# Expert weights of a two-layer mixture of experts: slot 1's first loads behind the first gather, its loads in a round one by one

## The chip, the cores and the metric

The kernel runs on one core of a Trainium2 chip. The time is that of the whole program on the device, in microseconds (us). A core has TensorE (PE, matrix products), VectorE (DVE), ScalarE (ACT), GpSimd (POOL) and SyncE (SP), each with its own instruction stream; SP, ACT and POOL also issue DMAs, and all DMAs of the core run on the same 16 DMA engines. Everything here is float32.

## The reference, cut to what matters

The program is two transformer-like blocks over 1024 tokens of width 1024. The change touches only the mixture of experts, which runs twice (`l` = 0 and 1, in the second block):

```python
def moe_ffn(h, w_rg, b_rg, w_re, b_re, w_gate, w_up, w_down):
    # routing: one of 4 groups, the 2 best of its 8 experts, a gate weight for each
    ...
    order = jnp.argsort(flat_e)              # 2048 (token, expert) pairs sorted by expert
    ...
    xb = h[row_tok].reshape(n_blocks, MOE_BLOCK, d)
    def expert_block(args):
        xblk, e = args
        hid = jax.nn.silu(xblk @ w_gate[e]) * (xblk @ w_up[e])
        return hid @ w_down[e]
    yb = lax.map(expert_block, (xb, block_e)).reshape(n_rows, d)
    return jnp.zeros_like(h).at[row_tok].add(yb * row_w[:, None])
```

There are 32 experts; each has 1024 x 512 gate and up matrices and a 512 x 1024 down matrix, together 6.3 MB.

## The kernel before

**Blocks and rounds.** The 2048 pairs are cut into blocks of 64 rows of one expert each. A *round* computes two blocks, one in *slot 0* and one in *slot 1*. The blocks are ordered so that slot 0 keeps its expert over several rounds (on average two), while slot 1's expert is loaded anew in every round. Layer 0 has 25 rounds and layer 1 has 24. A slot holds one expert as three parts of 2 MB each: half *a* and half *b* of the gate and up weights (each covers half of the contraction) and the *down* part. In the whole run ACT issues 98 half loads and 49 down loads for slot 1, SP 42 and 21 for slot 0.

**A round on PE** (`blocks_pe`): for slot 0, then slot 1: 16 matmuls on half a, 16 on half b (line 2314); then two transposes of slot 0's hidden rows (2321), eight transposes that turn the next round's gathered tokens (2298, `turn_x`), two transposes for slot 1, and 16 down matmuls for each slot (2331). PE waits for each half by itself (`self.wa`, `self.wb`) and for each down part (`self.wd`). When its last matmul on a part is done it raises `free_a`, `free_b` or `free_d`; each counts slot 0 and slot 1 in turn, from 2, so that `free_b >= 2*j+3` means that slot 0's half b is done in round `j`, and `2*j+4` slot 1's.

**Who loads what.** SP runs `blocks_sp` and reloads slot 0 as its parts come free. ACT has the loads of slot 1 in its own stream, in program order with its other work (`round_act`): Silu for slot 0, Silu for slot 1, a copy of half of the turned tokens (`copy_x`), the two half loads for the next round, the copy of slot 0's result, the two stores of it to `y_tok`, the two stores of slot 1's result (which DVE copies, `ye[1]`), the down load. POOL gathers the next round's 128 token rows from `h_tok` in DRAM (0.5 MB) once PE has turned the current ones (`blocks_pool`).

**Start of a layer.** Stages are closed by all four compute engines (`close`): the next stage begins on an engine when every engine has closed the last. In stage `m0_route` (`m1_route`), ACT ends `route_act` with slot 1's first three loads, each half held until slot 0's same half has landed (`landed[0], 32`), and closes the stage behind them. POOL's first gather is the first thing of the next stage, `m0_blocks`. SP does not take part in the closing; it issues slot 0's first loads as soon as the table of blocks is there (`m_tg`).

## Time and profile before

| | us |
|---|---|
| median of 3 runs | 4514.99 (4512.74 to 4518.06) |
| the profiled execution | 4513.96 |
| its span | 4512.1 |
| round stages, first to last expert matmul of slots and down, layer 0 | 2594.2 to 3236.3 |
| the same, layer 1 | 3829.3 to 4435.9 |

The page of the profile gives PE 88% of the span, DVE 32%, ACT 20%, POOL 3%. In its table of 40 slices, the two stages of experts (slices 23 to 29 and 34 to 40) are where the DMA engines are busiest, at 8 or 9 tenths in most slices. In the rows below, a line number such as L2314 is a line of the kernel before; L2267 issues a half load, L2272 a down load, L2348 a store, L2284 the gather. "Idle before" in brackets is the time the engine sat idle before the instruction, and who ended it.

### The profile page before, as it was taken

Reading aid. Unit: us, or ns where it says so; the run is one execution under the profiler, and the core shown is the slowest. Engines: PE = TensorE matmul, PEld = TensorE weight load, DVE = VectorE, ACT = ScalarE, POOL = GpSimd, SP = SyncE. Lnnn points to the kernel's source line nnn. Section 1 sums busy time; section 2 is a strip of 40 time slices with the busy share of each in tenths; the row PEclk is TensorE's granted clock in tenths of the full one; section 3 lists DMA queues with packets and bytes.
Section 4 is the critical chain, followed back from the end, with each engine's and each line's share of the span. In section 5 each row is a group of like instructions: output and inputs, shape, how many; then the busy total and the mean of one; then the engine's idle time right before and its main releaser. Section 6 shows DMA issues by size and latency. Waiting matters only on the chain. (4 is left out here: it accounts for less than half of the span.)

```text
span 4512.1 us, 48953 instructions
## 1 busy us (share of the span) xinstructions
PE 3960.7 (88%) x19350; PEld 1982.4 (44%) x19351; DVE 1440.6 (32%) x2699; ACT 898.9 (20%) x1891; POOL 122.8 (3%) x199
## 2 busy tenths in 40 slices
PE   4997888899998889999778599889799995999895
PEld 2564665454444554453554333333344443333333
DVE  2486666213204661431553311111231123111114
ACT  3003445102002331300451211111120012111111
POOL 0000000000000000000000000000100000000001
PEclk8998999999999999999999799999899997999997
DMA  6311223001100000110320389999811003899995
GB/s 248 121 38 38 95 101 125 28 22 38 55 37 19 1 1 28 47 47 37 133 102 2 153 322 375 404 401 406 316 36 38 37 20 158 322 395 379 408 404 208
DMA packets 81279, 693.44 MB, mean 154 GB/s; under 512 B 9696, under 2 KB 11560, under 8 KB 45408
## 3 DMA queue, kind: packets, MB, share of 16 engines
q10 hardware_dynamic: 39824, 342.78, 18.8%
q1 hardware_dynamic: 23168, 280.66, 15.5%
q0 software_dynamic: 18128, 67.77, 4.2%
q8 instruction: 114, 1.87, 0.2%
q14 instruction: 45, 0.37, 0.0%
HBM read 636.11 MB, written 55.05 MB: 153 GB/s over the span
## 5 line engine op out<-in xcount | busy, mean ns | idle before, releaser
L258 PE MATMUL banks<-arena 128*128 128x512 f32 (+2 forms) x4544 | 1750.1, 548 | 57.5 <-ACTq L137 30.4
L258 PEld LDWEIGHTS banks<-arena 128*128 128x128 f32 x4544 | 842.6, 191 | 959.0 <-issue 889.0
L2314 PE MATMUL banks<-arena 128*64 128x512 f32 x3136 | 708.0, 607 | 52.0 <-DMA arena<-in_w_gu 50.0
L2314 PEld LDWEIGHTS banks<-arena 128*64 128x64 f32 x3136 | 235.6, 140 | 515.3 <-issue 440.9
L2331 PE MATMUL banks<-arena 128*64 128x512 f32 x1568 | 371.2, 624 | 50.3 <-issue 50.3
L2331 PEld LDWEIGHTS banks<-arena 128*64 128x64 f32 x1568 | 115.4, 143 | 270.6 <-issue 270.6
L1511 PE MATMUL banks<-arena 128*64 128x128 f32 x1952 | 158.3, 285 | 83.8 <-DVE arena L1524 44.2
L937 DVE SCALAR_TENSOR_TENSOR arena<-arena 128x1024 f32<-128x1024 f32 x240 | 195.9, 877 | 0.2 <-DVEq L137 0.2
L1511 PEld LDWEIGHTS banks<-arena 128*64 128x64 f32 x1952 | 102.2, 136 | 136.6 <-ACT arena L1524 71.7
L299 DVE SCALAR_TENSOR_TENSOR arena<-banks,arena 128x512 f32<-128x512 f32 (+1 forms) x72 | 51.9, 721 | 337.4 <-PE banks L258 337.4
L2399 DVE COPY arena<-banks 128x512 f32<-128x512 f32 x49 | 33.9, 691 | 393.0 <-PE banks L2331 393.0
L2395 DVE COPY arena<-banks 128x256 f32<-128x256 f32 x98 | 41.1, 419 | 366.4 <-PE banks L2321 366.4
L1442 PE MATMUL banks<-arena 64*128 64x256 f32 (+2 forms) x768 | 131.4, 473 | 25.2 <-ACT arena L1613 15.6
L1491 PE MATMUL banks<-arena 128*128 128x128 f32 x976 | 150.1, 285 | 0.6 <-ACT arena L1613 0.6
L2391 DVE TENSOR_TENSOR arena<-arena,banks 128x256 f32<-128x256 f32 x98 | 40.7, 415 | 343.9 <-ACT arena L2355 343.9
L1239 PE MATMUL banks<-arena 128*128 128x128 f32 x800 | 109.4, 285 | 34.4 <-DVE arena L1330 34.4
L1557 DVE TENSOR_REDUCE arena<-banks 128x1 f32<-128x1024 f32 (+3 forms) x144 | 135.4, 940 | 13.0 <-PE banks L1442 9.3
L270 ACT ACTIVATE arena<-banks 128x512 f32<-128x512 f32 (+1 forms) x43 | 24.1, 559 | 577.5 <-PE banks L258 577.5
L1613 ACT ACTIVATE arena<-banks,arena 128x1024 f32<-128x1024 f32 (+3 forms) x144 | 135.3, 939 | 10.4 <-DVE arena L1559 9.4
L2355 ACT ACTIVATE arena<-banks 128x256 f32<-128x256 f32 x98 | 37.5, 383 | 495.2 <-PE banks L2314 495.2
L2355 ACT ACT_TABLE_LOAD x47 | 60.3, 1283 | 379.8 <-issue 379.8
L1491 PEld LDWEIGHTS banks<-arena 128*128 128x128 f32 x976 | 104.5, 141 | 54.1 <-issue 50.5
(341 smaller groups left out, 3105.8 us busy)
## 6 DMA issues: line engine op xcount, KB each, us to landing
arena<-in_w_gu ACTq DMA_DIRECT2D x98, 2048.0 KB, 13.9
arena<-in_w_dn ACTq DMA_DIRECT2D x49, 2048.0 KB, 17.2
arena<-in_w_gu SPq DMA_DIRECT2D x42, 2048.0 KB, 14.7
arena<-in_w_ada SPq DMA_DIRECT2D x24, 2048.0 KB, 7.3
arena<-in_w_dn SPq DMA_DIRECT2D x21, 2048.0 KB, 19.1
y_tok<-arena ACTq DMA_DIRECT2D x196, 128.0 KB, 9.9
y_tok<-arena POOLq DMA_DIRECT2D x1, 16384.0 KB, 45.2
arena<-in_ab_w_ada SPq DMA_DIRECT2D x6, 2048.0 KB, 10.4
```

The costliest lines, as they stand in the source:

```text
L258: last = pe.matmul(self.bank_of(g, n), lhsT, rhs, start=k == 0, stop=k == KT - 1)
L299: d.scalar_tensor_tensor(out=grp.dst, in0=src, scalar=grp.more["gate"], in1=grp.dst, op0=ALU.mult, op1=ALU.add).then_inc(proj_ev["D"], 1)
L937: d.scalar_tensor_tensor(out=out, in0=src, scalar=wt, in1=out, op0=ALU.mult, op1=ALU.add).then_inc(conv_n, 1)
L1239: last = pe.matmul(bank(7)[:, 0:V.shape[1]], self.PT[0:K, g % self.n_pt, 128 * j:128 * j + 128], V, start=g == mine[0] and j == 0, stop=g ...
L1442: ins = pe.matmul(banks[:, c0:c0 + k.shape[1]], q, k, start=True, stop=True)
L1491: ins = pe.transpose(self.tbank(g)[:, 128 * j:128 * j + 128], self.P[u % 2][s_][:, c0:c0 + P], ident)
L1511: ins = pe.matmul(bank(7)[64 * s_:64 * s_ + 64, 0:128], V, self.PT[g % len(self.PT)][:, 128 * j:128 * j + 128], start=g == mine[0] and j < ...
L1557: link(d.tensor_reduce(st[:, s_:s_ + 1], sc[:, 0:un["n"]], X_AXIS, ALU.max))
L1613: a.activation(self.P[i % 2][s_][:, 0:un["n"]], self.scores(s_)[:, 0:un["n"]], ACT.Exp, bias=st[:, 2 + s_:3 + s_], scale=un["scale"][s_][0 ...
L2314: last = pe.matmul(bank(2 + s_)[64 * h:64 * h + 64, :], xbT[:, k, 64 * s_:64 * s_ + 64], w_gu[s_][:, k, h], start=k == 0, stop=k == KT - 1 ...
L2331: last = pe.matmul(bank(6 + s_)[64 * h:64 * h + 64, :], hidT[:, s_, ch % 2, 64 * (ch // 2):64 * (ch // 2) + 64], w_dn[s_][:, ch, 512 * h:5 ...
L2355: a.activation(sg[:, s_], bank(2 + s_)[:, 0:256], ACT.Silu).then_inc(self.sg, 1)
```

## The change

In `route_act` the loads of slot 1 are taken out. They come at the head of the next stage, in `blocks_act`, once the first gather has landed (`xg >= 16`), without waits on slot 0's halves. In `round_act` half a is loaded when PE has freed it, between the two Silus; half b behind the second Silu; the down part between slot 0's stores and slot 1's, when PE has freed it (`free_d >= 2*j+4`).

```diff
@@ route_act
-                a.wait_ge(m_tg, l + 1)
-                e = self.expert(a, 0)
-                for part, landed in ((0, self.wa), (1, self.wb)):
-                    a.wait_ge(landed[0], 32)
-                    self.load_gu(a, 1, e, part)
-                self.load_dn(a, 1, e)
                 for tw in m_tw:
@@ round_act
-                for s_ in range(2):
-                    a.wait_ge(self.free_b, 2 * j + s_ + 3)
-                    a.activation(sg[:, s_], bank(2 + s_)[:, 0:256], ACT.Silu).then_inc(self.sg, 1)
+                a.wait_ge(self.free_b, 2 * j + 3)
+                a.activation(sg[:, 0], bank(2)[:, 0:256], ACT.Silu).then_inc(self.sg, 1)
+                if not last:
+                    a.wait_ge(self.free_a, 2 * j + 4)
+                    self.load_gu(a, 1, e, 0)
+                a.wait_ge(self.free_b, 2 * j + 4)
+                a.activation(sg[:, 1], bank(3)[:, 0:256], ACT.Silu).then_inc(self.sg, 1)
+                if not last:
+                    self.load_gu(a, 1, e, 1)
                 self.copy_x(a, "A", j + 1)
-                if not last:
-                    for part in range(2):
-                        self.load_gu(a, 1, e, part)
...
                 self.store_y(a, 0, j)
+                if not last:
+                    a.wait_ge(self.free_d, 2 * j + 4)
+                    self.load_dn(a, 1, e)
                 a.wait_ge(self.ye[1], j + 2)
                 self.store_y(a, 1, j + n)
-                if not last:
-                    self.load_dn(a, 1, e)
@@ blocks_act
+                e = self.expert(a, 0)
+                a.wait_ge(self.xg, 16)
+                for part in range(2):
+                    self.load_gu(a, 1, e, part)
+                self.load_dn(a, 1, e)
                 self.copy_x(a, "A", 0)
```

On ACT at the start of layer 0's expert stage, before: `moe0_w_half_a_slot0` counts slot 0's half a landed, `moe0_xt` the tokens turned, `stage_end` the closed stage.

```order
L2277 TENSOR_LOAD arena [waits moe_tg]
L2277 ISA x2
L2267 ISA [waits moe0_w_half_a_slot0]
L2267 DMA arena<-in_w_gu 128x4096
L2267 ISA [waits moe0_w_half_b_slot0]
L2267 DMA arena<-in_w_gu 128x4096
L2272 ISA
L2272 DMA arena<-in_w_dn 128x4096
L2244 TENSOR_LOAD arena [waits moe_tw1,moe_tw0,stage_end]
```

The same place now; the changed file's lines are numbered a little lower (2261 for 2267, 2266 for 2272).

```order
L2238 TENSOR_LOAD arena [waits moe_tw1,moe_tw0,stage_end]
L2238 ISA x2
L2373 TENSOR_LOAD arena
L2373 ISA x2
L2271 TENSOR_LOAD arena
L2271 ISA x2
L2261 ISA [waits moe0_xg]
L2261 DMA arena<-in_w_gu 128x4096
L2261 ISA
L2261 DMA arena<-in_w_gu 128x4096
L2266 ISA
L2266 DMA arena<-in_w_dn 128x4096
```

The three loads have moved from ahead of the stage's end to behind it, and from slot 0's halves to the gather as what releases them.

On ACT in the loop of rounds, before, from the first Silu to the down load:

```order
L2355 ACTIVATE arena<-banks 128x256 [waits moe0_free_b]
L2354 REGISTER_ALU
L2355 ACTIVATE arena<-banks 128x256 [waits moe0_free_b]
L2339 REGISTER_ALU
L2342 ACTIVATE arena<-banks 128x512 [waits moe0_xt]
L2267 ISA
L2267 DMA arena<-in_w_gu 128x4096
...
L2348 ISA [waits moe0_ye_dve]
L2348 DMA y_tok<-arena 64x512
L2348 ISA
L2348 DMA y_tok<-arena 64x512
L2272 ISA
L2272 DMA arena<-in_w_dn 128x4096
```

The same stretch now:

```order
L2348 ACTIVATE arena<-banks 128x256 [waits moe0_free_b]
L2350 REGISTER_ALU
L2261 ISA [waits moe0_free_a]
L2261 DMA arena<-in_w_gu 128x4096
L2353 ACTIVATE arena<-banks 128x256 [waits moe0_free_b]
L2261 ISA
L2261 DMA arena<-in_w_gu 128x4096
...
L2266 ISA [waits moe0_free_d]
L2266 DMA arena<-in_w_dn 128x4096
L2342 ISA [waits moe0_ye_dve]
L2342 DMA y_tok<-arena 64x512
```

Half a has moved ahead of the second Silu, half b ahead of the token copy, the down load ahead of slot 1's two stores. No other engine's instructions have moved.

## Rows read from the trace of the kernel before

**Rows 1.** The page: the span.

```profile
span 4512.1 us, 48953 instructions
```

**Rows 2.** Waits: engine and line, waited for; us in total, times, longest.

```profile
PE banks L2331 <- issue: 50.3, 17, 4.8
PE banks L2314 <- DMA arena<-in_w_gu: 50.0, 23, 4.8
```

**Rows 3.** Windows; columns: PE, PEld, DVE, ACT, POOL busy, PEclk, DMA share, GB/s.

```profile
2644.99:3158.76 513.77, 466.14 (x2162) 167.79 (x2160) 57.71 (x120) 64.86 (x100) 23.02 (x40) 0.97 0.97 396
3880.34:4365.88 485.54, 447.12 (x2054) 161.18 (x2052) 54.81 (x114) 61.62 (x95) 21.84 (x38) 0.96 0.96 391
3880.34:3955.86 75.52, 71.03 (x326) 24.86 (x324) 8.65 (x18) 9.73 (x15) 3.45 (x6) 0.95 0.92 374
4209.55:4261.20 51.65, 46.90 (x218) 17.43 (x216) 5.77 (x12) 6.49 (x10) 2.30 (x4) 0.97 0.99 407
3158.76:3236.50 77.74, 67.58 (x308) 25.39 (x304) 8.05 (x18) 8.45 (x14) 2.31 (x4) 0.96 0.89 372
4365.88:4436.70 70.82, 65.62 (x308) 22.99 (x304) 8.66 (x18) 8.45 (x14) 2.30 (x4) 0.98 0.86 347
2618.74:2641.14 22.40, 22.40 (x111) 8.08 (x109) 2.88 (x6) 3.24 (x5) 1.15 (x2) 1.00 0.83 327
```

**Rows 4.** Short windows of layer 1, same columns.

```profile
3867.00:3871.00 4.00, 4.00 (x26) 1.96 (x24) 1.77 (x4) 0.98 (x2) 0.81 (x2) 1.00 0.28 61
3942.00:3947.00 5.00, 5.00 (x30) 2.33 (x28) 1.77 (x4) 0.98 (x2) 1.15 (x2) 1.00 0.32 85
3906.00:3908.00 2.00, 2.00 (x8) 0.60 (x6) 0.00 (x0) 0.00 (x0) 0.00 (x0) 0.50 1.07 451
```

**Rows 5.** Timeline, start of layer 0's experts: start, us, engine, line, operation.

```profile
2562.62 0.19 DVE L2240 CAST arena<-banks 128x33 int32<-128x33 f32 x1 [1.71 <-PE banks L2054]
2562.68 1.03 SPq L2267 DMA_DIRECT2D arena<-in_w_gu  x2
2570.09 6.46 ACTq L2267 DMA_DIRECT2D arena<-in_w_gu  x2
2576.72 0.34 ACTq L2272 DMA_DIRECT2D arena<-in_w_dn  x1
2578.36 1.05 POOL L2284 DMA_INDIRECT arena<-h_tok,arena  x1 [0.87 <-POOL arena L2281]
2591.28 1.97 PE L2298 MATMUL banks<-arena 128*128 128x128 f32 x8 [28.77 <-DMA arena<-h_tok,arena]
2594.23 16.00 PE L2314 MATMUL banks<-arena 128*64 128x512 f32 x64 [0.98 <-DVE arena L2342]
```

**Rows 6.** Timeline, the same start in layer 1.

```profile
3798.48 0.19 DVE L2240 CAST arena<-banks 128x33 int32<-128x33 f32 x1 [1.71 <-PE banks L2054]
3829.31 16.27 PE L2314 MATMUL banks<-arena 128*64 128x512 f32 x64 [0.98 <-DVE arena L2342]
```

**Rows 7.** DMA issues from 3923 to 3924 us: KB each, median us to landing.

```profile
arena<-h_tok,arena POOLq DMA_INDIRECT x1, 12.2
```

**Rows 8.** The chain in order of time, one round of layer 1: start, us.

```profile
3876.66 13.73 PE banks L2314 x64
```

**Rows 9.** Timeline of the same round and the next one's stalls.

```profile
3890.44 0.38 ACT L2355 ACTIVATE arena<-banks 128x256 f32<-128x256 f32 x1 [6.48 <-PE banks L2314]
3891.82 0.86 ACTq L2267 DMA_DIRECT2D arena<-in_w_gu  x2
3898.89 3.60 PE L2314 MATMUL banks<-arena 128*64 128x512 f32 x16
3901.38 0.46 ACTq L2272 DMA_DIRECT2D arena<-in_w_dn  x1
3905.04 8.78 PE L2314 MATMUL banks<-arena 128*64 128x512 f32 x32 [2.55 <-DMA arena<-in_w_gu]
3915.76 5.35 PE L2314 MATMUL banks<-arena 128*64 128x512 f32 x16 [1.95 <-DMA arena<-in_w_gu]
```

## The prediction

> **What bounds the kernel now.** I read the page first, for the span [rows 1] and for the busiest engine, PE. The list of waits says where PE stands idle in the expert stages: PE waited 50.0 us in 23 places for halves of gate and up weights, and 50.3 us in 17 places in front of the down matmuls, where the profile names only "issue" [rows 2]; those stand in the middle of the 32 down matmuls, between slot 0's and slot 1's, so they are waits for slot 1's down part. The windows tell which resource is short. A round without a stall takes 22.40 us, with PE at 100% and DMA at 0.83 [rows 3]. From the first reload of slot 0 to the last, in both layers, the DMA engines are busy 0.97 and 0.96 of the time [rows 3]. So there are two kinds of time to win, and the reader should keep them apart: the start of each layer, where PE sits and nothing is short but order, and the steady part, where DMA is nearly full and only its idle 3 or 4% can be won.
>
> In the steady part SP reloads slot 0 every second or every third round (12 and 5 intervals). A two-round interval takes 51.65 us with DMA at 0.99 and 407 GB/s; a three-round one 75.52 us with DMA at 0.92 [rows 3]. PE would need 2 x 22.40 = 44.8 and 3 x 22.40 = 67.2 us. The idle DMA time of a three-round interval stands where slot 1 waits to be asked for: 3867 to 3871 us at a share of 0.28 and 3942 to 3947 at 0.32, so 2.9 and 3.4 us idle [rows 4]. Both end when the half loads behind the token copy start to move data. In the heavy round that follows, PE then waits 2.55 and 1.95 us, and each time runs its next matmuls at half the granted clock (0.50, the 1.2 GHz level) for a while: 16 matmuls take 5.35 us [rows 4, 9], where a quarter of 13.73 us is 3.43 [rows 8].
>
> **The start of a layer.** Before, ACT's first half load waits until slot 0's half a has landed (2570.09), its second until half b has, and the down load is issued at 2576.72. Only then does the stage close, and the gather goes out at 2578.36, 1.30 us after ACT's last issue ended (2577.06). It lands 12.9 us later, at 2591.28, behind the loads, and the first expert matmul comes 2.95 us after that, at 2594.23 [rows 5]. Now the last to close is DVE, whose last instruction ends at 2562.81. The same 1.30 us puts the gather at 2564.1. It now competes with slot 0's three loads alone. The nearest row is the gather in a light round, which had ACT's queue beside it and took 12.2 us [rows 7]; I take that, with 12.9 as the other end. So the gather lands at 2576.3, and the first expert matmul stands at 2579.3: 14.9 us earlier. Layer 1: DVE ends at 3798.67, so 3798.67 + 1.30 + 12.2 + 2.95 = 3815.1 against 3829.31, 14.2 us [rows 6]. Together 29.1 us, or 27.7 with 12.9.
>
> The cover that goes is that of slot 1's own loads: they start at about 2577, not at 2570. A load is 2.10 MB, which at 407 / 0.99 = 411 GB/s [rows 3] is 5.1 us. Slot 1's half b is the fifth load of the stage; with data moving from about 2564.7 (I allow 2 us behind SP's issue; no row here shows it), 5 x 5.1 + 1.3 for the gather ends at 2591.5. PE asks for it at 2579.3, plus slot 0's two halves (half of 13.73 plus the 16.27 - 13.73 of a slow start [rows 6, 8], 9.4 us), plus 3.43: 2592.1. That is just in time; I charge 0 to 3 us a layer and take 0.5. The down part would be there at 2596.6 and is asked for some 9 us after that half b. ACT issues three loads (about 0.5 us each) between the gather and its first token copy; PE's turning takes 1.97 us [rows 5], so they hide behind it; without that cover they would cost 1.5 us once a layer. **Start: -28 us** (-21 to -29).
>
> **In a round.** In the round of rows 8, slot 1's half a is free after three quarters of the 64 matmuls, at 3886.96. Its load was issued at 3891.82 and will be issued some 4.8 us earlier. Half b went 0.5 us behind it, at 3892.3; now it follows the second Silu (3890.44) by the 0.15 us that separated copy and load before: 1.7 us earlier. The down part was issued at 3901.38, behind two stores and DVE's copy; the last down matmul ends at about 3899.0 [rows 9], so 2.3 us earlier. A round's first load takes about 5 us of DMA, and it moves ahead by 4.8: what it does is fill the gap, and the whole train behind it comes that much sooner. In a round with stalls the gap closes altogether, since half a is asked for before PE waits for half b.
>
> What can that be worth? The idle DMA time between the first and the last reload is 0.03 x 513.77 + 0.04 x 485.54 = 34.8 us [rows 3]; more cannot be won there, since the bytes are the same. A three-round interval holds 0.08 x 75.52 = 6.0 us of it and a two-round one only 0.01 x 51.65 = 0.5. I count 80%, -28 us: in the light rounds of a three-round interval PE still needs its 22.40 us and DMA, with 0.83 of that to do, will idle a little. Of the stalls of 8.3 us in that interval (75.52 - 67.2), I expect 4 to 5 to stay, at slot 1's half b. Behind the last reload of a layer the stretches of 77.74 and 70.82 us [rows 3] stand about 13.5 and 6.5 us over what PE needs; the first has two other weight loads of the next stage on SP's queue. I count 2 and 3 us there. **Steady part: -33 us** (-15 to -48).
>
> **What is added or passed.** The wait on free_a on ACT has the second Silu behind it, which cannot start before slot 1's half b is done anyway, 3.43 us later: nothing. The wait on free_d has slot 1's stores behind it; DVE's copy that they need, which starts on the same signal, ends later still: nothing. Slot 1's stores now stand behind 2 MB on ACT's queue, so they land about 5 us later. DVE waits for them before its next copy of slot 1's result, and that copy follows 16 down matmuls (3.5 us) that themselves waited for this same down load; the stores, 0.26 MB behind it, take 0.6 us. Nothing, but with a margin of only about 3 us in a round that stalls there; beyond it each microsecond would reach ACT's next store and Silu, which has about 7 us of slack in turn. SP and POOL issue the same things; no queue is passed on them.
>
> **Sum.** 4513.96 for the profiled execution (span 4512.1 [rows 1], 1.9 us around it), minus 28, minus 33, is 4453; by rounding in the shares I say 4454. The median of the runs is 1.0 us above the profiled one, which is nothing here: a measurement of this kernel tells about 0.2%, 9 us, from no change.
>
> **Rivals.** *Only the start.* DMA is the bound and the idle slivers only move, for instance because the reordered loads arrive sooner than PE uses them and the wait passes to slot 0's parts. For it: the two-round intervals at 0.99. Against: the gaps of rows 4, which end with an issue that now comes 4.8 us sooner. Time 4513.96 - 28 = 4486. *Everything.* All 34.8 us of idle time go, the ends of both layers give 8 more and slot 1's half b is in time at the start (29): 4442, and down to 4434 if stalls that vanish take their slow matmuls with them beyond what the shares show. *Slower: half a steals from slot 0.* Where SP's and ACT's queues both hold loads they share the engines. In a heavy round ACT's half a now joins while SP's half b, which PE needs first, is still under way, for 4.8 us longer. At half the rate that puts SP's half b back by 2.4 us, and it was already 2.55 late at 3905.04 [rows 9]; with 1.9 us of slow matmuls that is 4.3 us in each of 19 heavy rounds, +82, less 28: 4568. It decides from 1.5 us lost in each heavy round on. Against it: before the heavy round the train has been moved ahead by those same 4.8 us, so ACT's queue is emptier when SP joins, and later parts gain what this one loses. *It doesn't do it.* If the gather, without the waits that staggered the loads, lands as late as before and ACT issues no sooner, because its stream is held elsewhere: about 4512.
>
> On that third case the Trainium skill has a rule, in "DMA: Bandwidth & Descriptors", section "Queues, rings and completion order": each DMA engine goes round-robin over the queues that hold work for it. By that rule the theft is real while both queues are full; whether it costs time is decided by the backlog, as above, and the profile of the change will show it. The same page's "Specifications" give about 358 GB/s as the HBM limit of a core; the two-round interval of rows 3 ran at 407, so the trace does not agree and the sum keeps to the trace. By that limit the interval's 21.0 MB would take 58.7 us, more than it did.
>
> **Chances.** Forecast (both parts, 4439 to 4472) 0.61; only the start 0.20; everything 0.12; theft 0.04; nothing 0.03. Faster by over 0.2% holds the first three, 0.93; within 0.2% 0.03; slower 0.04. The range reaches from "everything" to "only the start", 4434 to 4488.
>
> **What would show it.** Right: the first expert matmul of the stages within 17 us of SP's first load, where it was 31.6; the gather issued about 1.5 us behind SP's first issue; half a issued 0.1 us after three quarters of a round's 64 matmuls; three-round intervals of 70 to 72 us with DMA at 0.96 or more, two-round intervals of 51 us at 0.99; the waits before the down matmuls down from 50 us to under 20. Wrong: a first gather that takes over 15 us; a new wait of several microseconds in round 0 in front of slot 1's half b; waits of DVE for the stores of slot 1; two-round intervals of over 52 us with PE's longest waits in front of slot 0's half b.

## The result

| | us | |
|---|---|---|
| before, median of 4 runs | 4513.86 | 4510.16 to 4518.06 |
| after, median of 4 runs | 4441.66 | 4438.27 to 4446.76 |
| ratio | 0.9836 | 0.9824 to 0.9848 (95%) |
| forecast | 4454 | range 4434 to 4488 |

The change makes the kernel 1.6% faster: 72 us, where 60 were forecast. The spans of the two profiled executions differ by the same 72.0 us. Lines have moved in the kernel after: the gate and up matmuls stand at L2308 (before L2314), the down matmuls at L2325 (L2331), half loads at L2261, down loads at L2266, stores at L2342, the gather at L2278.

The page of the kernel after, span and costliest groups (answers to [rows 1]; columns: busy us, mean ns | idle before and what ended most of it):

```profile
span 4440.1 us, 48953 instructions
...
L2308 PE MATMUL banks<-arena 128*64 128x512 f32 x3136 | 719.6, 616 | 70.0 <-DMA arena<-in_w_gu 68.0
...
L2325 PE MATMUL banks<-arena 128*64 128x512 f32 x1568 | 349.2, 598 | 3.2 <-issue 3.2
```

Against [rows 2], the 50.3 us in front of the down matmuls have gone to 3.2 in one place. The waits for halves have grown from 50.0 to 68.0. So there are 29 us less waiting in all: nearly all of the waits for the down part have gone, and the halves take 18 us of them over.

The waits are not the whole gain in the rounds. From the first to the last expert matmul the two layers take 39 us less (1248.6 to 1209.4). Some 10 us of that are matmuls that run faster: the down matmuls are busy for 349.2 us instead of 371.2, those on the halves for 719.6 instead of 708.0. PE runs the matmuls behind a long wait at a granted clock of 0.50 for a while ([rows 4], 3906 to 3908 us), so a wait that goes takes its slow matmuls with it. The first expert matmuls of the two layers, 31 us earlier behind SP's first load, are most of the rest of the 72.

The windows of the kernel after, same columns as [rows 3]: first to last reload of slot 0 in each layer, a three-round interval, two two-round intervals, and the stretches behind the last reload:

```profile
2631.43:3124.46 493.03, 463.14 (x2162) 163.71 (x2160) 57.71 (x120) 64.44 (x101) 23.02 (x40) 0.97 0.99 413
3830.40:4298.83 468.43, 441.13 (x2054) 155.82 (x2052) 54.84 (x114) 61.64 (x96) 21.83 (x38) 0.97 0.98 406
3830.40:3904.15 73.75, 70.27 (x326) 24.79 (x324) 8.66 (x18) 9.75 (x16) 3.44 (x6) 0.95 0.94 385
4151.68:4198.85 47.17, 45.02 (x218) 16.09 (x216) 5.77 (x12) 6.44 (x11) 2.30 (x4) 1.00 1.01 424
2875.76:2926.54 50.78, 46.95 (x218) 16.41 (x216) 5.77 (x12) 6.50 (x11) 2.31 (x4) 0.97 1.01 426
3124.46:3199.77 75.31, 67.36 (x308) 24.67 (x304) 7.96 (x17) 8.33 (x14) 2.31 (x4) 0.95 0.86 360
4298.83:4365.09 66.26, 63.74 (x308) 22.69 (x304) 7.97 (x17) 8.01 (x14) 2.30 (x4) 1.00 0.83 347
```

The steady stretches fell from 513.77 and 485.54 us to 493.03 and 468.43, that is 37.8 us. The two-round interval fell too, to 47.17 us in the fourth row, though the prediction held it full at 51.65 and 0.99. Its row now says 1.01 and 424 GB/s where it said 0.99 and 407. That is 2% more share and 4% more bytes a second.

The timeline of the start of layer 0's experts, then of layer 1's (answers to [rows 5, 6]):

```profile
2562.86 0.20 DVE L2234 CAST arena<-banks 128x33 int32<-128x33 f32 x1 [1.71 <-PE banks L2054]
2562.91 1.04 SPq L2261 DMA_DIRECT2D arena<-in_w_gu  x2
...
2564.19 1.05 POOL L2278 DMA_INDIRECT arena<-h_tok,arena  x1 [0.87 <-POOL arena L2275]
...
2575.35 1.16 ACTq L2261 DMA_DIRECT2D arena<-in_w_gu  x2
...
2578.17 8.89 PE L2308 MATMUL banks<-arena 128*64 128x512 f32 x32 [0.98 <-DVE arena L2336]
...
2587.82 3.65 PE L2308 MATMUL banks<-arena 128*64 128x512 f32 x16 [0.75 <-DMA arena<-in_w_gu]
...
2593.03 3.65 PE L2308 MATMUL banks<-arena 128*64 128x512 f32 x16 [1.56 <-DMA arena<-in_w_gu]
```

```profile
3760.99 1.02 SPq L2261 DMA_DIRECT2D arena<-in_w_gu  x2
...
3777.26 13.52 PE L2308 MATMUL banks<-arena 128*64 128x512 f32 x48 [0.98 <-DVE arena L2336]
...
3792.00 3.65 PE L2308 MATMUL banks<-arena 128*64 128x512 f32 x16 [1.22 <-DMA arena<-in_w_gu]
```

The first expert matmul comes 2578.17 - 2562.91 = 15.3 us behind SP's first load in layer 0, where it was 31.6, and 3777.26 - 3760.99 = 16.3 us in layer 1, where it was 31.3. The DMA issue at 2564.19 in the timeline is the gather; its own row, against [rows 7]:

```profile
arena<-h_tok,arena POOLq DMA_INDIRECT x1, 11.0
```

Then a round without a stall, and a heavy one (answers to [rows 8, 9]):

```profile
2605.18 13.90 PE L2308 MATMUL banks<-arena 128*64 128x512 f32 x64
2605.53 0.34 ACTq L2266 DMA_DIRECT2D arena<-in_w_dn  x1
...
2615.83 0.35 ACTq L2261 DMA_DIRECT2D arena<-in_w_gu  x1
...
2619.13 0.38 ACT L2353 ACTIVATE arena<-banks 128x256 f32<-128x256 f32 x1 [6.48 <-PE banks L2308]
2619.28 0.34 ACTq L2261 DMA_DIRECT2D arena<-in_w_gu  x1
```

```profile
3848.95 10.47 PE L2308 MATMUL banks<-arena 128*64 128x512 f32 x48
...
3862.89 6.50 PE L2308 MATMUL banks<-arena 128*64 128x512 f32 x16 [3.48 <-DMA arena<-in_w_gu]
```

Half a is issued 10.65 us after the first matmul of the round. The start of the same kind of round before is read from the same view here, the timeline, which puts it 0.17 us ahead of the chain of [rows 8]:

```profile
3876.49 13.90 PE L2314 MATMUL banks<-arena 128*64 128x512 f32 x64
```

There half a was issued 3891.82 - 3876.49 = 15.33 us into the round, so it is now asked for 4.7 us sooner. Half b goes out at 14.10 us, and the down part 0.35 us into the next round. The heavy round has one wait, at its last 16 matmuls, which are slot 1's half b.

The windows of a light round of layer 1 in which a gap is left (answers to [rows 4]); the gap now ends with half a's load, issued 10.65 us into the round:

```profile
3886.00:3888.00 2.00, 2.00 (x12) 0.71 (x10) 0.00 (x0) 0.00 (x0) 0.00 (x0) 1.00 0.13 48
3888.00:3890.00 2.00, 2.00 (x12) 0.65 (x10) 0.00 (x0) 0.00 (x0) 0.00 (x0) 1.00 0.53 106
```

Cut into slots of 2 us, the steady stretches (first to last reload of slot 0) show how much each kernel left unused. I take a slot that moves under 200 GB/s as one in which the queues ran dry; between 200 and 380 I expect slots with the small stores or with a short gap. "Lost" is the time that the missing bytes would take at 430 GB/s, the rate of a full slot (the median of the slots above 380 is 432 before and 426 after). The waits of PE, by the quarter of the 64 gate and up matmuls or the half of the down matmuls that they precede, are summed from the timeline.

| | slots under 200 (lost us) | 200 to 380 (lost us) | waits at slot 0's half b | slot 1's halves | slot 0's down | slot 1's down | waits in all |
|---|---|---|---|---|---|---|---|
| before | 28 (43.8) | 85 (43.3) | 13.5 | 36.6 | 0 | 50.3 | 100.4 |
| after | 10 (15.9) | 47 (21.0) | 0 | 68.0 | 0 | 3.2 | 71.2 |

### The profile page after: what moved, and what is told of

The parts are those of the page before. It is cut to its first block and busy times, and to the rows that moved or that the text cites. A ratio compares the mean times of both kernels' runs of the same rounds, so it can differ in the third digit from the quotient of the medians.

```text
span 4440.1 us, 48953 instructions
## 1 busy us (share of the span) xinstructions
PE 3953.8 (89%) x19350; PEld 1975.0 (44%) x19351; DVE 1441.2 (32%) x2699; ACT 898.7 (20%) x1891; POOL 121.7 (3%) x199
## 5 line engine op out<-in xcount | busy, mean ns | idle before, releaser
L2308 PE MATMUL banks<-arena 128*64 128x512 f32 x3136 | 719.6, 616 | 70.0 <-DMA arena<-in_w_gu 68.0
L2308 PEld LDWEIGHTS banks<-arena 128*64 128x64 f32 x3136 | 231.5, 142 | 548.2 <-issue 455.8
L2325 PE MATMUL banks<-arena 128*64 128x512 f32 x1568 | 349.2, 598 | 3.2 <-issue 3.2
L2325 PEld LDWEIGHTS banks<-arena 128*64 128x64 f32 x1568 | 108.9, 137 | 208.5 <-issue 208.5
L1511 PEld LDWEIGHTS banks<-arena 128*64 128x64 f32 x1952 | 101.9, 136 | 137.3 <-ACT arena L1524 71.7
L270 ACT ACTIVATE arena<-banks 128x512 f32<-128x512 f32 (+1 forms) x43 | 24.1, 559 | 580.3 <-PE banks L258 580.3
L1524 ACT ACTIVATE arena<-banks 128x512 f32<-128x512 f32 (+1 forms) x160 | 90.6, 566 | 168.5 <-PE banks L1491 167.1
L278 ACT ACTIVATE arena<-banks 128x512 f32<-128x512 f32 (+1 forms) x68 | 38.0, 559 | 424.1 <-PE banks L258 424.1
## 6 DMA issues: line engine op xcount, KB each, us to landing
y_tok<-arena ACTq DMA_DIRECT2D x196, 128.0 KB, 13.9
```

Source lines behind the costliest of these rows:

```text
L1511: ins = pe.matmul(bank(7)[64 * s_:64 * s_ + 64, 0:128], V, self.PT[g % len(self.PT)][:, 128 * j:128 * j + 128], start=g == mine[0] and j < ...
L1524: last = eng.tensor_copy(o, s_) if which == "D" else eng.activation(o, s_, ACT.Copy)
L2308: last = pe.matmul(bank(2 + s_)[64 * h:64 * h + 64, :], xbT[:, k, 64 * s_:64 * s_ + 64], w_gu[s_][:, k, h], start=k == 0, stop=k == KT - 1 ...
L2325: last = pe.matmul(bank(6 + s_)[64 * h:64 * h + 64, :], hidT[:, s_, ch % 2, 64 * (ch // 2):64 * (ch // 2) + 64], w_dn[s_][:, ch, 512 * h:5 ...
```

## The experiments

The theory at this point: two parts that don't touch each other, a start worth some 28 us and loads in the rounds that fill DMA gaps. Gains in us "by the ratio" are the ratio's distance from 1 times 4514. The rivals: that one part does it all, that the stores play a role, and that the order in which slot 0's and slot 1's parts share the engines matters. All twelve runs are told here.

**The start alone.** The two hunks on `route_act` and `blocks_act`, the round as before:

```diff
@@ route_act
-                a.wait_ge(m_tg, l + 1)
-                e = self.expert(a, 0)
-                for part, landed in ((0, self.wa), (1, self.wb)):
-                    a.wait_ge(landed[0], 32)
-                    self.load_gu(a, 1, e, part)
-                self.load_dn(a, 1, e)
@@ blocks_act
+                e = self.expert(a, 0)
+                a.wait_ge(self.xg, 16)
+                for part in range(2):
+                    self.load_gu(a, 1, e, part)
+                self.load_dn(a, 1, e)
                 self.copy_x(a, "A", 0)
```

> The start alone: slot 1's first loads behind the first gather, the rounds as before. If the two parts of the change are independent, the traces give 14 and 13 us for the two layers, so 27 us less than before (ratio 0.994), the first expert matmul 15 to 16 us behind SP's first load, and steady intervals as before (DMA 0.97 and 0.96). Rival: since the stages are bound by DMA later on, what is won at the start is given back before the end: under 10 us less, ratio above 0.998.

Measured: 4488.75 us, ratio 0.9936 (0.9918 to 0.9955). The first matmul comes 15.2 us behind SP's first load. The steady stretches stay as they were, 517.19 and 485.02 us at 393 and 391 GB/s. The start is worth 29 us by the ratio, where 27 were expected; the rival, under 10, falls.

**The rounds alone.** The hunk on `round_act`, the start as before:

```diff
@@ round_act
-                for s_ in range(2):
-                    a.wait_ge(self.free_b, 2 * j + s_ + 3)
-                    a.activation(sg[:, s_], bank(2 + s_)[:, 0:256], ACT.Silu).then_inc(self.sg, 1)
+                a.wait_ge(self.free_b, 2 * j + 3)
+                a.activation(sg[:, 0], bank(2)[:, 0:256], ACT.Silu).then_inc(self.sg, 1)
+                if not last:
+                    a.wait_ge(self.free_a, 2 * j + 4)
+                    self.load_gu(a, 1, e, 0)
+                a.wait_ge(self.free_b, 2 * j + 4)
+                a.activation(sg[:, 1], bank(3)[:, 0:256], ACT.Silu).then_inc(self.sg, 1)
+                if not last:
+                    self.load_gu(a, 1, e, 1)
                 self.copy_x(a, "A", j + 1)
-                if not last:
-                    for part in range(2):
-                        self.load_gu(a, 1, e, part)
...
                 self.store_y(a, 0, j)
+                if not last:
+                    a.wait_ge(self.free_d, 2 * j + 4)
+                    self.load_dn(a, 1, e)
                 a.wait_ge(self.ye[1], j + 2)
                 self.store_y(a, 1, j + n)
-                if not last:
-                    self.load_dn(a, 1, e)
```

> The rounds alone: loads in a round as in the change, the start as before. Independent parts: 45 us less than before (72 less 27; ratio 0.990), waits in front of the down matmuls under 5 us in total. Rival: the two parts need each other (the earlier train of loads helps only with the earlier start): 30 us less or not even that.

Measured: 4471.42 us, ratio 0.9903 (0.9883 to 0.9923), 44 us, where 45 were expected. The waits in front of the down matmuls are 1.0 us. The starts take 82.4 and 82.1 us to the first reload, as before. The windows of the steady stretches:

```profile
2643.58:3137.32 493.74, 463.95 (x2162) 163.85 (x2160) 57.76 (x120) 64.86 (x101) 23.03 (x40) 0.97 0.99 411
3855.54:4321.47 465.93, 436.91 (x2054) 154.79 (x2052) 54.85 (x114) 61.63 (x96) 21.84 (x38) 0.98 0.98 408
```

They are those of the whole change to within 3 us. 29 and 44 make 73, and the whole is 72 to 74: the two parts are independent and add up.

**Only half a ahead of the second Silu**, everything else as before:

```diff
@@ round_act
-                for s_ in range(2):
-                    a.wait_ge(self.free_b, 2 * j + s_ + 3)
-                    a.activation(sg[:, s_], bank(2 + s_)[:, 0:256], ACT.Silu).then_inc(self.sg, 1)
+                a.wait_ge(self.free_b, 2 * j + 3)
+                a.activation(sg[:, 0], bank(2)[:, 0:256], ACT.Silu).then_inc(self.sg, 1)
+                if not last:
+                    a.wait_ge(self.free_a, 2 * j + 4)
+                    self.load_gu(a, 1, e, 0)
+                a.wait_ge(self.free_b, 2 * j + 4)
+                a.activation(sg[:, 1], bank(3)[:, 0:256], ACT.Silu).then_inc(self.sg, 1)
                 self.copy_x(a, "A", j + 1)
                 if not last:
-                    for part in range(2):
-                        self.load_gu(a, 1, e, part)
+                    self.load_gu(a, 1, e, 1)
```

> In a round only half a is moved (ahead of the second Silu); half b, the down load and the start stay. Theory of the gap (the gain is the idle DMA time in front of a round's first load): half a alone takes most of it, 25 to 35 us less than before (ratio 0.992 to 0.9945). Theory of the stores (DMA is slow while the stores to y_tok run alone, which the earlier down load prevents): half a alone gives 15 us or less, ratio above 0.9965.

Measured: 4464.89 us, ratio 0.9882 (0.9866 to 0.9899), 53 us. The steady stretches are 490.66 and 464.85 us. I had expected 25 to 35 us, a part of the rounds' gain, and it is no less than all of it (44 us for the three edits together, with overlapping intervals). Below 200 GB/s stand 6 slots (9.0 us lost). PE's waits total 72.6 us, in other places than in the kernel after: 43.8 at slot 0's half b, 20.5 at slot 1's, 8.3 at slot 1's down part.

**Only the down part ahead of slot 1's stores**, everything else as before:

```diff
@@ round_act
                 self.store_y(a, 0, j)
-                a.wait_ge(self.ye[1], j + 2)
-                self.store_y(a, 1, j + n)
                 if not last:
+                    a.wait_ge(self.free_d, 2 * j + 4)
                     self.load_dn(a, 1, e)
+                a.wait_ge(self.ye[1], j + 2)
+                self.store_y(a, 1, j + n)
```

> In a round only the down load is moved ahead of slot 1's two stores; the halves and the start stay. Theory of the gap: the down load comes 2.3 us sooner but the first load of a round does not, so it only shortens the waits for the down part: 5 to 12 us less than before. Theory of the stores: about half of the rounds' gain, 20 us or more less.

Measured: 4503.82 us, ratio 0.9975 (0.9963 to 0.9986), 11 us. The waits in front of the down matmuls vanish (50.3 to 0), and those at the halves rise from 50.0 to 92.4 us. In front of slot 1's half a alone stand 89.2 of them. The wait has moved; only 8 of the 50 us are gone. The time lies in the 5 to 12 us of the theory of the gap; that of the stores asked for 20 or more.

**The start and half a together, nothing else.** The first and the third edit:

```diff
@@ route_act, blocks_act
...
@@ round_act
...
+                a.wait_ge(self.free_b, 2 * j + 3)
+                a.activation(sg[:, 0], bank(2)[:, 0:256], ACT.Silu).then_inc(self.sg, 1)
+                if not last:
+                    a.wait_ge(self.free_a, 2 * j + 4)
+                    self.load_gu(a, 1, e, 0)
+                a.wait_ge(self.free_b, 2 * j + 4)
+                a.activation(sg[:, 1], bank(3)[:, 0:256], ACT.Silu).then_inc(self.sg, 1)
                 self.copy_x(a, "A", j + 1)
...
```

> The start and half a; half b and the down load stay behind the token copy and behind slot 1's stores. If half b's and the down load's moves are worth nothing, this is level with the whole change or a little better: ratio 0.982 to 0.984. If they are worth something once the start is early, it is slower than the change: ratio 0.985 to 0.987.

Measured: 4441.86 us, ratio 0.9836 (0.9816 to 0.9856). That is the whole change, to the fourth digit. Moving half b and the down part forward adds nothing that the interval, some 9 us to either side, would show once half a has moved.

**Both halves between the second Silu and the token copy.** The kernel before with one block moved:

```diff
@@ round_act
+                if not last:
+                    for part in range(2):
+                        self.load_gu(a, 1, e, part)
                 self.copy_x(a, "A", j + 1)
-                if not last:
-                    for part in range(2):
-                        self.load_gu(a, 1, e, part)
```

> The kernel before with both halves ahead of the token copy, behind the second Silu: the round's first load comes 1.2 us sooner, not 4.8, and half b 1.7 us sooner. If the gain grows with how much sooner the round's first load is issued (half a alone gave 49 us for 4.8 us), this gives a quarter of it, 10 to 15 us less than before (ratio 0.9967 to 0.9978). Rival: closing any gap at all is what counts, or half b's own move: 30 us or more less.

Measured: 4513.90 us, ratio 0.9993 (0.9983 to 1.0002): nothing, where 10 to 15 us were expected. Half a is issued 14.09 us into a round without a stall instead of 15.33, some 1.2 us sooner. The timeline of a round with a stall shows what that order leaves open, and the windows of 2 us behind it the gap:

```profile
2882.26 5.35 PE L2314 MATMUL banks<-arena 128*64 128x512 f32 x16 [3.87 <-DMA arena<-in_w_gu]
...
2887.79 0.86 ACTq L2267 DMA_DIRECT2D arena<-in_w_gu  x2
```

```profile
2886.00:2888.00 2.00, 2.00 (x12) 0.75 (x9) 0.00 (x0) 0.34 (x1) 0.00 (x0) 1.00 0.63 270
2888.00:2890.00 2.00, 2.00 (x14) 1.15 (x14) 1.77 (x4) 0.64 (x2) 0.18 (x2) 1.00 0.61 139
```

PE waits for slot 1's half b, and no half is asked for until the 16 matmuls behind it are through; by then the engines run dry. The two windows also show how little the share tells: at 0.63 and 0.61 of the engines busy, 270 and 139 GB/s were moved. The kernel before has the same behind its stall at 3915.76 [rows 9], in two windows of its trace:

```profile
3920.00:3922.00 2.00, 2.00 (x15) 1.10 (x12) 0.48 (x2) 0.38 (x1) 0.00 (x0) 1.00 0.35 147
3922.00:3924.00 2.00, 2.00 (x12) 0.80 (x12) 1.29 (x3) 0.60 (x1) 0.68 (x2) 1.00 0.58 115
```

The prediction had put numbers on the gaps of the light rounds alone [rows 4].

**Half a ahead of the second Silu, but 3 us later.** The third edit, with six Silus of no use in front of the load. Their counts go on the semaphore of the Silus, so DVE's wait on it changes with them:

```diff
@@ round_act (half a ahead of the second Silu, and)
+                a.wait_ge(self.free_a, 2 * j + 4)
+                for i in range(6):
+                    a.activation(sg[:, 1], xbT[:, 0:2].rearrange("p k n -> p (k n)"), ACT.Silu).then_inc(self.sg, 1)
+                    a.wait_ge(self.sg, 8 * j + i + 2)
                 if not last:
                     self.load_gu(a, 1, e, 0)
@@ DVE
-                        d.wait_ge(self.sg, 2 * j + s_ + 1)
+                        d.wait_ge(self.sg, 8 * j + 7 * s_ + 1)
```

> Before, with half a's load ahead of the second Silu as in the run with half a alone (ratio 0.988), but six Silus of no use (256 elements a partition, each waited for) stand in front of that load. They hold it back by about 3 us: in a light round it goes out about at the end of the 64 matmuls, where the run with both halves behind the second Silu had it (ratio 1.000); in a round with a stall at slot 1's half b it still goes out before or during the stall. The outputs are unchanged. Theory A (what counts is that a load is queued on ACT's ring while PE stands in the stall, so that the engines don't run dry when the awaited half has landed): most of the gain stays, ratio 0.986 to 0.991, steady stretches 491 to 500 and 465 to 472 us, DMA 408 GB/s or more. Rival B (what counts is the 4.8 us in a light round, and the run with both halves behind the Silu gained nothing because its lead there was too short): the gain goes with them, ratio 0.996 to 1.001, steady stretches over 508 and 480 us. Between 0.991 and 0.996 both hold a part.

Measured: 4499.19 us, ratio 0.9956 (0.9944 to 0.9968), with runs spread from 4487.29 to 4514.76; the profiled execution is the slowest of them. A stall and what follows it, timeline and windows:

```profile
2875.04 2.65 ACT L2357 ACTIVATE arena<-arena 128x256 f32<-128x256 f32 x6 [3.05 <-PE banks L2314]
2877.85 0.35 ACTq L2267 DMA_DIRECT2D arena<-in_w_gu  x1
2879.46 6.00 PE L2314 MATMUL banks<-arena 128*64 128x512 f32 x16 [4.47 <-DMA arena<-in_w_gu]
```

```profile
2884.00:2886.00 2.00, 2.00 (x12) 0.78 (x11) 0.13 (x1) 0.38 (x1) 0.00 (x0) 0.95 1.07 459
2886.00:2888.00 2.00, 2.00 (x15) 1.05 (x15) 1.64 (x4) 0.60 (x1) 0.33 (x2) 1.00 0.92 393
```

The edit does what it was built for: half a is asked for during the stall (2877.85, 1.6 us before it ends), and the engines stay full behind it. Yet the time falls by 20 us, not by 53. In the profiled execution slots under 200 GB/s drop from 28 to 15, but those from 200 to 380 rise from 85 to 95, PE's waits total 93.2 us against 100.4, and the steady stretches take 513.34 and 483.37 us, hardly less than before. That execution, at 4514.76 us, won nothing at all; of the ones that won up to 27 us there is no trace. So closing the dry stretch behind the stall shown isn't enough, and theory A as I had put it falls. By the rule laid down beforehand (0.991 to 0.996: both hold a part) the run stands next to rival B: more of the gain goes with the 3 us of lead than stays without them. Set side by side, with half a's issue after the round's first matmul in a round without a stall:

| half a at | lead over before | gain by the ratio |
|---|---|---|
| 15.33 us (before) | 0 | 0 |
| 14.09 (both halves after the Silu) | 1.2 | 3 |
| 13.33 (delayed) | 2.0 | 20 |
| 10.65 (half a alone) | 4.7 | 53 |

These leads hold for rounds without a stall. In a round with a stall at slot 1's half b the last two kernels ask for half a before the stall ends and the first two only behind the matmuls that follow it; in the delayed kernel's stall above that is 9 us earlier (half b, which goes where both halves went before, is issued at 2886.88). So two things change from row to row, and the table doesn't part them.

**The stores with one row, before and after.** In each of these two kernels a store writes 1 of its 64 rows; 63 of 64 rows of the experts' output are left out. The first is the kernel before, the second the one after:

```diff
@@ store_y
-                    a.dma_start(t["y_tok"][bass.ds(blk * BLK, BLK), 512 * h:512 * h + 512],
-                                y_sb[64 * h:64 * h + 64, s_]).then_inc(self.yw[s_], 16)
+                    a.dma_start(t["y_tok"][bass.ds(blk * BLK, 1), 512 * h:512 * h + 512],
+                                y_sb[64 * h:64 * h + 1, s_]).then_inc(self.yw[s_], 16)
```

> The kernel before, but each store to y_tok writes one of its 64 rows: the same waits and issues, 1.0 MB less to move in every round pair and no stretch in which the stores move alone. The other 63 rows are left as they were. Theory of the stores: before suffers from stores that move slowly while nothing else does; without them it comes down to near the change's time, 50 us or more less than before (ratio under 0.989). Theory of the gap: only the bytes go, 5% of them in the steady part, at most 25 us less (ratio 0.9945 or above).

> The change with the same one-row stores; 63 of 64 rows are left out as in the run beside it. Theory of the gap: the difference between this run and the kernel before with one-row stores stays 55 to 75 us. Theory of the stores: it shrinks to the start's 27 us and little more, 30 to 40 us.

Measured: 4483.44 us, ratio 0.9923 (0.9901 to 0.9946), and 4381.92 us, ratio 0.9703 (0.9681 to 0.9726). Steady stretch of layer 0, first the kernel before with one-row stores, then the kernel after:

```profile
2643.86:3149.80 505.94, 468.04 (x2162) 163.65 (x2160) 57.72 (x120) 64.93 (x101) 23.10 (x40) 0.97 0.91 382
```

```profile
2629.68:3096.93 467.25, 453.36 (x2162) 161.52 (x2160) 57.70 (x120) 64.86 (x101) 23.02 (x40) 0.99 0.98 413
```

Without the bytes of its stores the kernel before wins only 33 us, more than the 25 of the theory of the gap and less than the 50 of the theory of the stores. Its DMA share falls to 0.91, and 52 slots lie under 200 GB/s (89.8 us lost). So it was not bound by the amount of data alone, but by when loads were asked for. The kernel after wins 60 us from the same saving, and the change is worth 101 us on top of small stores, more than the 55 to 75 that the theory of the gap expected and far from the 30 to 40 of the theory of the stores. The theory that the change gains because of the stores falls.

**SP's down part held until slot 1's half a has landed.** The kernel after, with one wait more on SP. It tests whether the order in which the two queues share the engines matters: slot 1's half a is needed before slot 0's down part.

```diff
@@ blocks_sp
                     sp.wait_ge(self.free_d, pos + 1)
                     sp.sem_inc(self.passed, 1)
+                    sp.wait_ge(self.wa[1], pos * 8 + 16)
+                    sp.sem_inc(self.passed, 1)
                     self.load_dn(sp, 0, e)
```

> The change, and SP holds slot 0's down load until slot 1's half a has landed, so that it doesn't share the engines with slot 1's half b, which PE needs about 5 us sooner. If the order of the loads matters, the stall in front of slot 1's half b (3.5 us and slow matmuls in each three-round interval) shrinks: 5 to 15 us less than the change (ratio 0.980 to 0.9825). Rival: only the sum of bytes matters, and SP's queue now idles between landing and issue: the change's ratio of 0.9836, or above.

Measured: 4418.94 us, ratio 0.9781 (0.9763 to 0.9799) to the kernel before. This is the fastest full kernel here, 23 us under the changed one. Its steady stretches, its waits, and one of them:

```profile
2635.93:3120.28 484.35, 458.16 (x2162) 173.26 (x2160) 57.69 (x120) 64.90 (x101) 23.02 (x40) 0.98 1.00 419
3823.93:4277.61 453.68, 433.11 (x2055) 165.84 (x2053) 54.78 (x114) 61.56 (x96) 21.84 (x38) 0.98 1.00 416
```

```profile
PE banks L2327 <- issue: 52.7, 19, 5.5
...
PE banks L2310 <- DMA arena<-in_w_gu: 8.0, 7, 1.8
```

```profile
3929.81 8.78 PE L2327 MATMUL banks<-arena 128*64 128x512 f32 x32 [2.30 <-issue]
```

The waits for halves fall from 68.0 to 8.0 us and those before down matmuls (L2327 here) rise from 3.2 to 52.7: 38.9 us in 16 places in front of slot 0's down part, which is what is held, and 13.9 in 3 places in front of slot 1's. In all 60.8 us instead of 71.2, and only 2 slots under 200 GB/s (3.7 us lost). The gain is larger than the 5 to 15 us that were expected. SP's first loads of a layer come out of the same loop, so the hold acts there too.

**The same wait, shorter.** SP holds its down part only until slot 0's own half b has landed:

```diff
@@ blocks_sp
                     sp.wait_ge(self.free_d, pos + 1)
                     sp.sem_inc(self.passed, 1)
+                    sp.wait_ge(self.wb[0], 16 * j + 32)
+                    sp.sem_inc(self.passed, 1)
                     self.load_dn(sp, 0, e)
```

> The change, with slot 0's down load held until slot 0's own half b has landed, 3 to 6 us instead of about 7 behind the point where PE frees it. The longer hold took the stall from slot 1's half b (68 to 8 us) and put 53 us in front of slot 0's down matmuls. If both are one queue's order, the shorter hold lies between: waits of 30 to 45 us in sum over both places and the time at or below the longer hold's (ratio 0.976 to 0.979). Rival: the gain comes from ACT's queue having the engines alone until half a has landed, and the shorter hold gives half of it back: 0.980 to 0.982.

Measured: 4431.28 us, ratio 0.9804 (0.9789 to 0.9819), 10 of the 23 us. Its steady stretches are 479.98 and 458.59 us, in sum 938.6, and those of the longer hold 938.0. Between the reloads the short hold is worth as much. What it gives away is at the ends: 71.6 and 72.4 us to the first reload instead of 68.4 and 68.8, and 78.4 and 72.9 us behind the last instead of 73.5 and 69.8, together 15 us. The start has a visible cause. The short hold lets SP's first down part go right beside slot 1's first halves, which ACT issues at 2576.13, and PE then waits at slot 1's half b; the long one keeps it back until half a is there. SP's down load and PE's wait, short hold and then long hold:

```profile
2577.49 0.33 SPq L2268 DMA_DIRECT2D arena<-in_w_dn  x1
2595.26 5.35 PE L2310 MATMUL banks<-arena 128*64 128x512 f32 x16 [3.76 <-DMA arena<-in_w_gu]
```

```profile
2588.24 0.33 SPq L2268 DMA_DIRECT2D arena<-in_w_dn  x1
2596.08 3.65 PE L2310 MATMUL banks<-arena 128*64 128x512 f32 x16 [1.14 <-DMA arena<-in_w_gu]
```

The first expectation fails: the waits are 62.5 us in sum, not 30 to 45, and the ratio is just above its range. The rival's ratio is met, but not for its reason, since the steady stretches lost nothing. Why the stretches behind the last reload are longer stays open.

**The start without the wait on the gather.** The kernel after without one line:

```diff
@@ blocks_act
                 e = self.expert(a, 0)
-                a.wait_ge(self.xg, 16)
                 for part in range(2):
```

> The change without ACT's wait for the first gather: slot 1's first loads go out as soon as the stage opens, beside the gather, and share the engines with it. If the order behind the gather matters, the gather takes 14 to 16 us instead of 11 to 12, the first expert matmul comes 3 to 5 us later in each layer, slot 1's half b is in time, and the sum is 2 to 8 us more than the change (ratio 0.984 to 0.9855). Rival: only closing the stage early matters, and the change's ratio of 0.9836 stays or improves.

Measured: 4446.37 us, ratio 0.9846 (0.9831 to 0.9861). The timeline of layer 0's start, and the gather's landing:

```profile
2563.39 1.04 SPq L2261 DMA_DIRECT2D arena<-in_w_gu  x2
...
2565.81 1.16 ACTq L2261 DMA_DIRECT2D arena<-in_w_gu  x2
...
2584.08 16.10 PE L2308 MATMUL banks<-arena 128*64 128x512 f32 x62 [0.98 <-DVE arena L2336]
```

```profile
arena<-h_tok,arena POOLq DMA_INDIRECT x1, 16.4
```

With slot 1's loads beside it the gather takes 16.4 us instead of 11.0, and the first matmul comes 20.7 us behind SP's first load instead of 15.3. In return slot 1's half b is in time. The first reload comes 3.5 and 3.0 us later than in the kernel after (71.97 and 72.36 us against 68.52 and 69.41). The time fits the 2 to 8 us expected, but its interval holds the change's 0.9836 as well; that the order matters is shown by the two starts and not by the total.

## Why the prediction was right, and where its sizes were off

**The start: -28 forecast, -26.7 found.** From SP's first load to the first reload layer 0 went from 82.3 to 68.5 us and layer 1 from 82.3 to 69.4. In layer 0 the gather was issued 1.28 us after SP's first load, and landed after 11.0 us, not 12.2 (11.5 in layer 1). So the first matmul came 15.3 us behind SP's first load, where 16.6 were forecast (2579.3 - 2562.68). But slot 1's loads were later than I had them: 0.75 us of wait at its half a and 1.56 at its half b in layer 0, 1.22 at half b in layer 1, where I had charged 0.5. The two errors have opposite signs and nearly cancel. The 2 us that I allowed before data move were no measurement; in the first 2 us behind SP's first issue the kernel before moves 131 GB/s. ACT's three issues before its first token copy cost nothing visible: the copy starts at 2577.23, together with DVE's.

**The steady part: -28 forecast, -37.8 found.** This is the term of the sum that was mis-sized. Its direction and its cause were right: half a's load was asked for 4.7 us sooner (I had said 4.8), the gaps filled, and half a alone brings all of the gain. Two things were wrong in its size.

First, the cap. I took "the idle DMA time between the first and the last reload is ... 34.8 us; more cannot be won there, since the bytes are the same", from the shares. 37.8 were won, and the kernel with SP's down part held wins 61.3 (999.31 - 938.03). The share doesn't measure bytes: in these traces engines count as busy while they move few. Rows of before already said so: at a share of 0.28 the engines moved 61 GB/s [rows 4], where 0.28 of 407 / 0.99 would be 115. The bound that holds is one by bytes: in full slots these kernels move some 430 GB/s, so by this estimate (1 - 396/430) x 513.77 + (1 - 391/430) x 485.54 = 40.6 + 44.0 = 85 us were to be had. After the change 19.5 + 26.1 = 46 us are left, and with SP's down part held 12.4 + 14.8 = 27.

Second, the places. I gave 6.0 us of room to each of the 5 three-round intervals and 0.5 to each of the 12 two-round ones. It came the other way round: the three-round intervals fell from 375.9 to 364.5 us in all, 11.4 us, and the two-round ones from 623.4 to 596.9, 26.5 us. By bytes, a two-round interval of the kernel before loses 2.4 to 4.2 us and not 0.5. The 12 of them held 9 slots under 200 GB/s and 35 from 200 to 380; the change leaves none and 19. In 15 of those 35 the share read 0.95 or more, so it showed them as full. A three-round one lost 8 to 10 us and still loses 6 to 8: of its two dry places, behind the stall and in the light round, the change closes the first. Before half a is asked for in a light round (3886 to 3890 us) the engines run dry as before. So the three-round intervals take 71.8 to 73.8 us, at a share of 0.94 in the one shown, where 70 to 72 at 0.96 were forecast, and the two-round ones 47 to 51.5, where 51 were. That the sum of 28 came as near to 37.8 as it did is therefore partly luck: too much was forecast for the three-round intervals (about 24 against 11.4) and too little for the two-round ones (about 5 against 26.5).

**The ends: -5 forecast, -5.9 found**, 77.5 to 75.3 and 70.0 to 66.3 us from the last reload to the last expert matmul. The three terms make 70.4 of the 72 us; the rest lies outside the stretches from SP's first load to the last expert matmul.

**The details.** "The waits before the down matmuls down from 50 us to under 20": 3.2. Half b was said to matter by 1.7 us and the down part by 2.3 us of lead; with half a moved they are worth nothing (start and half a alone: 0.9836, as the whole). The down part alone is worth 11 us and moves 50 us of waits to the halves. DVE's wait for slot 1's stores didn't appear, though the stores' median time from issue to landing went from 9.9 to 13.9 us.

**The rivals.** *Only the start* would have been 4486, and the kernel with only the start measures 4489: its price was right, its claim wrong, since the rounds bring 44 us more. *Everything* (4442) gives the number measured, 4441.66, but not for its reason. It supposed that the steady part would be full; the slots show that 39 of its 85 us were taken. *Theft by half a* (4568) has a true mechanism without its cost. With half a moved alone, the waits at slot 0's half b rise from 13.5 to 43.8 us. But those at slot 1's down part fall from 50.3 to 8.3 at the same time. In the whole change, slot 0's half b shows no wait at all. In the full kernels the order of the loads moves the waits from place to place, while their sum goes with how much the engines left unused (100.4 us at 87 lost before, 71.2 at 37 after, 60.8 at 19 with the long hold). *It doesn't do it* fell with the first timeline.

**What stays open.** Why 1.2 us of lead bring 3 us and 2.0 bring 20 wasn't settled, nor how much of it belongs to the rounds with a stall. The delayed load closes the dry stretch behind the stall shown; 15 slots under 200 GB/s remain elsewhere, and its six runs spread over 27 us where the kernel after spreads over 8. That the pattern of stalls changes from run to run is a guess that no run here tests.

## What to carry to other kernels

A share of busy DMA time near 1 does not say that nothing is left: divide the bytes of the stretch by the rate of its fullest slots, and look at slots of 2 us to find where the queues run dry, behind stalls above all. On a bound queue, ask for the next load as soon as its buffer is free, ahead of anything on the issuing engine that waits for later work; here a later load in the same round added nothing that could be measured once the first was early. After that, order the queues by need: holding slot 0's down part, which is used later, until slot 1's half a, which is used sooner, had landed was worth another 23 us here.

## What was not expected of the hardware

The two-round intervals shown have a DMA share of 0.99 at 407 GB/s in the kernel before and 1.01 at 424 to 426 in the one after; 2% of share stand for over 4% of bytes. The gather of the first 128 rows took 11.0 us beside SP's loads alone and 16.4 beside SP's and ACT's. Removing nearly all bytes of the stores, 0.52 MB a round, brought the kernel before 33 us and the changed one 60: the same bytes cost more where the engines are fuller.
